# final_norm_g loaded as one row and spread by TensorE into two banks

## The reference

```python
xf = x.astype(jnp.float32) + gate1 * mix
h = _rmsnorm(xf, norm2_g) * (1.0 + scale2) + shift2
xf = xf + gate2 * _moe(h, ...)
...
y_prompt = _rmsnorm(xp, final_norm_g)
y_sample = _rmsnorm(xs, final_norm_g)

def _rmsnorm(x, g):
    return x * rsqrt(mean(x * x, axis=-1) + EPS) * g
```

## Time and profile before

| what | value |
|---|---|
| median of 3 runs | 809.95 us (808.82 to 810.01) |
| the profiled execution | 809.93 us |
| its span in the trace | 808.0 us |
| TensorE busy | 767.9 us, 95% |
| VectorE busy | 374.4 us, 46% |
| ScalarE busy | 239.7 us, 30% |
| GpSimd busy | 22.4 us, 3% |
| HBM read | 280.67 MB, 351 GB/s over the span |

### The profile page before, as it was taken

The page is one execution under the profiler, slowest core; times in us unless marked ns, Lnnn a source line. Parts: engine busy times, 40 slices in busy tenths (PEclk is TensorE's granted clock), DMA queues, the critical chain, the costliest instruction groups (busy, mean ns, idle before and its releaser), DMA issues.

```text
span 808.0 us, 13131 instructions
## 1 busy us (share of the span) xinstructions
PE 767.9 (95%) x5410; PEld 522.1 (65%) x5410; DVE 374.4 (46%) x765; ACT 239.7 (30%) x427; POOL 22.4 (3%) x22
## 2 busy tenths in 40 slices
PE   5999999999999999999999899899999999999975
PEld 3689897899999999954445344454554664543522
DVE  1266999889998666463222212122222111221114
ACT  3254747354355444131111111111111111121102
POOL 1000010100100100200000000000000000000000
PEclk9999999999999999999999989999999999999989
DMA  9999798633534399799999999999999999999995
GB/s 351 408 395 346 280 410 299 208 106 105 196 119 145 118 311 417 312 411 424 363 423 427 427 430 430 428 428 432 426 428 428 432 427 428 432 427 429 426 423 238
DMA packets 63342, 284.73 MB, mean 352 GB/s; under 512 B 4880, under 2 KB 7216, under 8 KB 43568
## 3 DMA queue, kind: packets, MB, share of 16 engines
q1 hardware_dynamic: 62848, 282.67, 86.6%
q10 hardware_dynamic: 432, 1.18, 0.4%
HBM read 280.67 MB, written 3.16 MB: 351 GB/s over the span
## 4 chain that ended last, share of the span: by engine, by line
PE 75%; DMA 13%; SPq 5%; DVE 4%; issue 1%; ACT 1%; POOL 0%; DVEq 0%; POOLq 0%; ACTq 0%
PE bank L2291 18%; DMA slot_pair<-in_w_expert_gate_up 10%; PE bank L2344 8%; PE bank L1837 6%; PE bank L1839 5%; PE bank L1842 5%; PE bank L2197 4%; PE bank L2169 4%; PE bank L1786 3%; SPq L663 3%; PE bank L1859 2%; DMA x_back<-x_kept 2%; PE bank L1861 2%; PE bank L1863 2%; SPq L673 2%; PE bank L1934 2%
## 5 line engine op out<-in xcount | busy, mean ns | idle before, releaser
L2291 PE MATMUL bank<-slot_pair,xg 128*32 128x512 f32 (+2 forms) x1040 | 192.9, 625 | 15.0 <-DMA slot_pair<-in_w_expert_gate_up 15.0
L2291 PEld LDWEIGHTS bank<-slot_pair,xg 128*32 128x32 f32 (+2 forms) x1040 | 62.5, 131 | 139.0 <-issue 123.8
L2344 PE MATMUL bank<-slot_dn,act_t 128*64 128x512 f32 (+2 forms) x488 | 91.2, 596 | 4.7 <-ACT act_t L1059 4.7
L1625 DVE SCALAR_TENSOR_TENSOR act_r<-bank,w_slot,sil 128x256 f32<-128x256 f32 x26 | 12.6, 484 | 174.9 <-ACT sil L1057 174.9
L1057 ACT ACTIVATE sil<-bank 128x256 f32<-128x256 f32 x26 | 10.0, 385 | 189.9 <-PE bank L2291 189.9
L1639 DVE TENSOR_TENSOR y_lo<-bank,y_hi 128x512 fp32r<-128x512 f32 x52 | 36.0, 692 | 65.3 <-ACT y_hi L1072 65.3
L1173 DVE TENSOR_TENSOR ring_lo<-ring,ring_hi 128x1024 fp32r<-128x1024 f32 x44 | 52.9, 1218 | 15.6 <-ACT ring_hi L838 15.5
L2344 PEld LDWEIGHTS bank<-slot_dn,act_t 128*64 128x64 f32 (+2 forms) x488 | 29.4, 127 | 47.2 <-issue 46.4
L1072 ACT ACTIVATE y_hi<-bank 128x512 fp32r<-128x512 f32 x52 | 31.1, 597 | 87.9 <-PE bank L2344 84.6
L1234 DVE SCALAR_TENSOR_TENSOR conv<-upad,dw,conv 128x256 f32<-128x256 f32 x120 | 52.8, 513 | 0.0
L838 ACT ACTIVATE ring_hi<-ring 128x1024 fp32r<-128x1024 f32 x44 | 44.6, 1054 | 24.6 <-PE bank L1863 19.0
(11 more groups left out here) (322 smaller groups left out, 1162.8 us busy)
## 6 DMA issues: line engine op xcount, KB each, us to landing
slot_pair<-in_w_expert_gate_up SPq DMA_DIRECT2D x39, 2048.0 KB, 27.3
slot_dn<-in_w_expert_down SPq DMA_DIRECT2D x62, 1024.0 KB, 27.0
slot_pair<-in_w_expert_gate_up SPq DMA_DIRECT2D x50, 1024.0 KB, 11.8
ring<-in_w_in SPq DMA_DIRECT2D x15, 2048.0 KB, 10.0
ring<-in_w_ada SPq DMA_DIRECT2D x12, 2048.0 KB, 10.1
ring<-in_w_proj_hgrn SPq DMA_DIRECT2D x2, 2048.0 KB, 8.3
ring<-in_w_out SPq DMA_DIRECT2D x2, 2048.0 KB, 11.2
ring<-in_w_proj_conv SPq DMA_DIRECT2D x1, 2048.0 KB, 8.9
```

Of the source, the lines that this page charges most:

```text
L2291: ins = mm(bank[2 + b][row:row + width, :], xg[:, k, c:c + width], w[:, k % 4, :], start=(k == 0), stop=(k == KD - 1))
L2344: ins = mm(out[row:row + width, :], act_t[:, c, row:row + width], weights[item][:, c, h * 512:(h + 1) * 512], start=(c == 0), stop=(c == 1))
```

## The change

final_norm_g is loaded as one row of 4 KB into one partition. After the transposes of x1, TensorE waits for the row and for two of VectorE's residual adds, and multiplies a column of ones with the row, 512 values at a time, into the two banks that held sample 0's sums. `x1_ready` goes to 5 when both are done. VectorE waits for that in place of the load, and reads the gain from the banks, for both samples.

```diff
-        fin_g = at("fin_g", 120, [P, D])
+        fin_row = at("fin_row", 120, [1, D])
...
+        fin_gain = y_acc[0]
...
-        sq_summed, x1_ready = sem("x1_squares_summed"), sem("x1_by_token_ready")
+        sq_summed, x1_ready = sem("x1_squares_summed"), sem("x1_by_token_then_final_gain_ready")
...
-            sp.dma_start(fin_g[:, :], A["final_norm_g"].rearrange("(a d) -> a d", a=1).broadcast_to([P, D])).then_inc(s_x, 16)
+            sp.dma_start(fin_row[:, :], A["final_norm_g"].rearrange("(a d) -> a d", a=1)).then_inc(s_x, 16)
...
             def final_norm(s, halves=range(2)):
                 dve.wait_ge(f_rms, s + 1)
-                dve.wait_ge(s_x, 48)
+                dve.wait_ge(x1_ready, 5)
                 for hf in halves:
                     c = slice(hf * 512, (hf + 1) * 512)
-                    V.scalar_tensor_tensor(fin[:, s, c], fin[:, s, c], rmsf[:, s:s + 1], fin_g[:, c], ALU.mult, ALU.mult).then_inc(out_done, 1)
+                    V.scalar_tensor_tensor(fin[:, s, c], fin[:, s, c], rmsf[:, s:s + 1], fin_gain[hf][:, :], ALU.mult, ALU.mult).then_inc(out_done, 1)
...
                 pe.wait_ge(s_x1_back, 16)
                 for j in range(4):
                     x1_to_tokens(j)
+                pe.wait_ge(s_x, 48)
+                pe.wait_ge(x2_done, 2)
+                for hf in range(2):
+                    ins = mm(fin_gain[hf][:, :], ones[0:1, :], fin_row[0:1, hf * 512:(hf + 1) * 512], start=True, stop=True)
+                ins.then_inc(x1_ready, 1)
```

## The result

The changed kernel took 811.38 us (median of 22 runs, 809.76 to 813.09) against 809.79 for the kernel before (22 runs, 808.47 to 812.25). The ratio is 1.0016, with a 95% interval from 1.0010 to 1.0022: 0.8 to 1.8 us slower. 809.6 had been forecast, with a range of 808.7 to 810.6: the time lies 0.8 above it, and it went up where 0.3 us down had been forecast.

What follows compares the result with a forecast made beforehand. Weight streaming fills 800 us untouched by the change; in the last 12 us VectorE's queue, then the sums, roots and scaling, bound it. Late start +0.15 and hold -0.45 give -0.30: 809.93 to 809.6 us, range 808.7 to 810.6.

Steps and rivals of the forecast that it cites:

- The load: Loading final_norm_g as 4 KB instead of 512 KB, behind x1 in the queue: frees nothing, and the row lands in time.
- TensorE's start and the matmuls: After the transposes: start 800.35, two matmuls 1.98 us at full clock, first scaled half 0.15 us late.
- PSUM reads: Four scaled halves reading the gain from a bank: no added cost, bounds -0.01 to +0.01 us each.
- The hold: GpSimd's second root, held beside VectorE's two-SBUF second scaled half: 1.00 us becomes 0.55, gaining 0.45 us.
- VectorE's end: VectorE's last scaled halves: +0.15 late start and -0.45 hold make them 0.30 us sooner.
- the last landing moves along: Output DMAs at the end: halves stay 0.67 us or more apart, so the last landing shifts with VectorE's gain.
- Nothing is queued behind it on TensorE: TensorE's new wait and spreading after the transposes: no further work behind them is delayed.
- The one for the other side: Rival between transposes and first scaled half: TensorE at half clock becomes the bound, 811.3 us (811.7 with hold); chance 0.05.
- x1's landing isn't late: Before the residual adds: x1's first transposed block is ready before 799.00, so VectorE's queue sets the end up to 801.5.
- Something outside the sum: Rival: weight streaming or TensorE's clock around 780 moves the kernel over 1.6 us; chance 0.04 down, 0.04 up.
- the change moves the time by less than 1.6 us: Whole kernel: time stays within about 0.2%, 1.6 us, of no change; chance 0.90.

Runs made afterwards that it cites:

- the full load: Changed kernel with the load of before (512 KB, final_norm_g written to all 128 partitions): 1.0024 against the kernel before, tail 11.1 us.
- the second measurement: The changed kernel measured once more, unaltered, on the chip of the first follow-ups: 1.0026 against the kernel before, tail 11.1 us.
- the trace with the output on ScalarE's queue: Changed kernel with the fourth output half issued from ScalarE's queue instead of SP's: 1.0021 against the kernel before, tail 11.2 us.
- the six slow traces: Changed kernel, its full-load, repeated and ScalarE-output runs; kernel before with late matmuls alone (1.0015) or a late TensorE wait alone (1.0028).

## Why the prediction was wrong

**The load: right.** Nothing for 508 KB less (0.9995).

**TensorE's start and the matmuls: right.** 800.94 less 0.54 is 800.40 (forecast 800.35), 1.95 us (1.98) at full clock. VectorE saw the bank 0.11 us later, not 0.04, so the first half was 0.24 late in place of 0.15, and followed GpSimd's first root by 0.32, not by 0.1 to 0.2. A size, not a cause.

**PSUM reads: right.** 745 ns. The Trainium skill's dearer PSUM sources ("VectorE: DVE Perf Modes", the section on the errata) are not seen in this form of instruction.

**The hold: right.** 0.55 or 0.56 us with one tensor in PSUM in each trace that has it so, 0.99 or 1.00 in each that has both in SBUF, whichever tile it was. That was the half of the Trainium skill's rule on shared ports ("SBUF — State Buffer", "Who interferes with whom") that no row of before could show; the trace agrees.

**VectorE's end: right.** 0.2 us sooner, forecast 0.30; the missing 0.1 is for the most part the late sight of the bank.

**The step that failed** is one sentence on outputs, "the last landing moves along", and one on TensorE, "Nothing is queued behind it on TensorE". No instruction was queued behind it, true. But the *end of its program* was, with a jump, and the instruction packets that follow it go through the same 16 engines as the outputs. So a new wait on TensorE was priced at nothing beyond VectorE's own delay, and the last landing at 2.0 us behind its issue as before; it took 3.8. The page lists such packets for what they are (queues of kind "instruction"), and the window of 801 to 804 had one, from 802.4 to 803.7, just ahead of the outputs' data. They were not read. The price in the tail is 10.6 to 11.2 less 8.85, some 1.8 to 2.4 us. With the 0.2 us that VectorE did gain (0.30 had been forecast) that is +1.6 to +2.2, against +1.3 by the ratio of the runs (1.0016), and +1.9 and +2.1 of the full load and the second measurement (1.0024, 1.0026).

**The rivals.** The one for the other side was placed on TensorE, but on the wrong side of it: its clock ahead of VectorE's scaling, not its end behind. Its clock stayed at 1.00. That x1's landing isn't late held for the trace that was read, not for all: in the trace with the output on ScalarE's queue VectorE waited 0.49 us for it, and in two more about 0.2. "Something outside the sum" had 0.04 for slower, but what happened was inside. The statement that the change moves the time by less than 1.6 us held (+1.3, chance 0.90), but not for its reasons: a gain of 0.2 and a loss of about 1.8 that the sum didn't have happened to stay below it.

**What stays open.** What keeps one engine from the outputs for about a microsecond before the packet starts in four of the six slow traces (in the other two the packet itself lasts 1.5 and 1.7); why the second packet follows the first by 3.1 us in one trace and 4.7 in another; which instructions it holds; and what sent SP's fourth issue to 1.44 us in one trace of two.

## What to carry to other kernels

When work is added to an engine that was done, ask not only who waits for the result but what the engine's program does when it ends: a jump there was followed by instruction packets here, and in the last microseconds they met the outputs. Read the DMA queues of kind "instruction" in small windows near the end, and the share of one engine (0.06) after the others stop. And measure a tail from an anchor near the change, since runs that spread over microseconds hide tenths that one trace shows plainly.

## What was not expected of the hardware

- A 16 KB instruction packet took 1.0 to 1.7 us of one of 16 DMA engines, and an output of 256 KB, landing in 2.0 us without it, took up to 4.3 us: it lands with the slowest engine.
- A jump on TensorE with results at hand left it idle for 2.7 and 3.0 us between two matmuls, in the midst of a scatter.
- GpSimd's root took 1.00 us beside a VectorE operation on two SBUF tensors, and moving one of the two tensors to PSUM ends it altogether: 1.00 to 0.56 us, for an operation of the same length.
- One row by 128 columns of ones, 512 values of fp32: 1.95 us for two such matmuls, about as long as the estimate from 128 rows (1.98).
